# Stick-breaking weights turned in 32x32 blocks by VectorE and placed by ScalarE, in a two-layer streaming encoder

## The chip, the cores and the metric

The kernel runs on one NeuronCore of a Trainium2 chip. The metric is the device time of one execution, in microseconds (us); lower is better. In what follows PE is TensorE, DVE is VectorE, ACT is ScalarE, POOL is GpSimd and SP is SyncE.

## What is computed

Two layers over 512 tokens of width 2048, in float32. Layer A mixes a gated linear recurrence with an attention into 256 memory tokens; layer B mixes a stick-breaking attention of 12 heads (keys and values computed once, from the stream after layer A) with the same kind of memory attention. The change touches the stick-breaking attention alone:

```python
z = jnp.einsum('bhqd,bhkd->bhqk', q_blk, kh).astype(jnp.float32) * scale
log_beta = jax.nn.log_sigmoid(z)
log_keep = jnp.where(mask, jax.nn.log_sigmoid(-z), 0.0)
later = lax.cumsum(log_keep, axis=3, reverse=True) - log_keep
w = jnp.where(mask, jnp.exp(log_beta + later), 0.0)
return jnp.einsum('bhqk,bhkd->bhqd', w.astype(vh.dtype), vh)
```

The mask keeps keys that stand strictly before the query.

## The kernel before, in words

**Products.** A float32 product is made as three passes of PE (`three_passes`, L2126 to L2128) over operands that are each split in a high part (`..._hi`, written by ACT as a copy) and a low part (`..._lo`, the difference, written by DVE). Weights come from HBM in slabs of 512 rows by 512 columns, double-buffered: SP loads `w_raw`, ACT's `split` writes `w_hi` in two halves once the slab before the one that PE is in has been left (`slab_done`), DVE's `split` writes `w_lo`, and PE's `slab` waits for each piece (`lo_ready`) before its first of four token tiles. A slab on PE is four quarters (`t` 0 to 3) of 12 matmuls with 512 moving columns. Between quarters, `hooks` put other work on PE.

**The stick-breaking stage.** A loop of three turns (`Fori(0, NPAIR)`) runs eight slabs each, the gate columns and the next query columns of layer B's input projection, and beside them four heads: head `h` belongs to slabs (slots) `2h` and `2h+1`. For a head:

- `stick_scores` on PE writes the scores `z` of four query tiles to the PSUM tensor `aux`, tile `t` with its `128(t+1)` keys only. The first head's scores stand at quarter 1 of slot 0; those of the next heads stand straight behind the value products of the head ahead.
- ACT (L1222, L1223) writes `keep` and `beta`, the two sigmoids of `z`, for the four tiles.
- DVE (L1970 to L1977) masks the diagonal blocks, runs the reversed running product over `keep` and multiplies it into `beta`: these are the weights, with queries on partitions. `w_ready` counts the tiles.
- `stick_transposed` on PE (L2473) turns the ten 128x128 blocks of the weights that are not empty (four, three, two and one for the key blocks 0 to 3), into three banks of `aux`. It stands at quarter 1 (first head) or 0 (others) of the odd slot and raises `wt_done`.
- ACT (L1214) writes `wt_hi` from `aux` in pieces of 512, 512 and 256 columns, DVE (L1960) writes `wt_lo`.
- `stick_values` on PE (L2484), two quarters after the turn, waits for all of `wt_lo` and makes twelve products with the values, then the next head's scores follow.

**The order on ACT and DVE.** It is written out by hand and is the program's order; a wait holds all that stands behind it on its engine. In an even slot ACT first splits the next slab (waiting for PE's progress), then makes the head's eight sigmoids and issues the load of the next head's keys and values (`load_kv`); in slot 4 `gate_sigmoid` follows (L858, one instruction of 2048 columns). In an odd slot ACT makes `wt_hi`, then splits. DVE does the same in step: in an even slot `w_lo`, then the scan steps of the head; in an odd slot `wt_lo`, `w_lo`, then what the slot adds: in slots 3 and 7 the copies of the finished projection out of PSUM (`gate_out`, `branch_out`: L1514, L1510), in slot 5 the gate products, and in each odd slot the head's output after `o_done`.

**Sums of weights.** POOL, far from this stage's own data, makes sums of blocks of the output weights in HBM by accumulating DMAs (`move`, L621), counted in four semaphores `sums_made[n]`, one for each quarter `n` of this work; SP waits for them before it loads those sums.

## Time and profile before

| | |
|---|---|
| time, median of 3 runs | 1468.43 us (1468.14 to 1469.89) |
| span of the profiled execution | 1466.5 us |
| time of the profiled execution itself | not given apart from its span |
| PE busy | 1458.0 us, 99% of the span |
| DVE busy | 997.5 us, 68% |
| ACT busy | 716.3 us, 49% |
| the stick-breaking loop | three turns, one of them in the window of 1027 to 1134 us |
| PE, in the window of 1027 to 1134 us | 107.00 us busy of 107 |
| DVE, ACT in that window | 65.72 us, 38.42 us |

The span reaches from the first to the last instruction of the profiled execution; the runs' times hold also what lies around it, 1.9 us by the median. Busy time counts an engine as busy while any of its instructions is in flight. Matmuls overlap, so the duration of one is longer than the distance to the next; for PE the distance of the starts is what an instruction costs. In the chain of waits each piece of time belongs to what the end of the program waited for.

### The profile page before, as it was taken

What the parts mean: (1) busy time and instruction counts of PE and PEld (TensorE: products, weight loads), DVE (VectorE), ACT (ScalarE), POOL (GpSimd) and SP (SyncE); (2) the same over time, 40 slices, a digit from 0 to 9 for tenths busy, and PEclk for the clock granted to TensorE, in tenths of its full rate; (3) what the DMA queues carried; (4) which work ended last, traced back from release to release, by engine and by line L of the source; (5) the groups of instructions that cost most, each with busy time, mean ns of one, the idle gap of its engine ahead of it and who ended that gap; (6) DMA issues with size and microseconds to landing.
All of it is one profiled execution on the core that took longest, in us unless ns stands there. A gap on an engine that the chain in (4) does not pass through costs nothing.

```text
span 1466.5 us, 18207 instructions
## 1 busy us (share of the span) xinstructions
PE 1458.0 (99%) x6842; PEld 1221.7 (83%) x6842; DVE 997.5 (68%) x1317; ACT 716.3 (49%) x1066; POOL 122.8 (8%) x184
## 2 busy tenths in 40 slices
PE   9999999999999999999999999999999999999998
PEld 7888888888888888888888888888888888888886
DVE  6775568465576896856579676556566566578987
ACT  6764544444544645763325654433333433455465
POOL 0001111111110000000010001111111011000000
PEclk9999999999999999999999999999999999999999
DMA  9877788777886987477989876687888888858853
GB/s 344 290 287 225 159 215 228 174 235 158 212 251 165 323 323 260 155 262 282 358 326 372 291 224 219 244 218 196 230 241 244 202 239 208 226 188 329 315 200 144
DMA packets 154189, 357.97 MB, mean 244 GB/s; under 512 B 7824, under 2 KB 23440, under 8 KB 150032
## 3 DMA queue, kind: packets, MB, share of 16 engines
q1 hardware_dynamic: 103824, 205.98, 40.3%
q0 software_dynamic: 29376, 102.77, 28.3%
q10 hardware_dynamic: 20928, 48.41, 9.0%
q8 instruction: 38, 0.62, 0.2%
q14 instruction: 23, 0.19, 0.0%
HBM read 310.99 MB, written 113.25 MB: 289 GB/s over the span
## 4 chain that ended last, share of the span: by engine, by line
PE 99%; DMA 0%; SPq 0%; ACT 0%; issue 0%; DVE 0%; ACTq 0%
PE main L2128 25%; PE main L2127 25%; PE main L2126 25%; PE aux L2127 6%; PE aux L2126 6%; PE aux L2128 6%; PE aux L2484 2%; PE aux L2473 1%; DMA w_raw<-in_w_mem_kv 0%; PE aux L2270 0%; PE main L2178 0%; PE aux L2178 0%; PE main L2199 0%; PE main L2202 0%; PE main L2205 0%; PE aux L2220 0%
## 5 line engine op out<-in xcount | busy, mean ns | idle before, releaser
L2126 PE MATMUL main<-act_hi,w_hi 128*128 128x512 f32 x1216 | 475.3, 391 | 0.0
L2127 PE MATMUL main<-act_lo,w_hi 128*128 128x512 f32 x1216 | 473.6, 389 | 0.0
L2128 PE MATMUL main<-act_hi,w_lo 128*128 128x512 f32 x1216 | 473.6, 389 | 0.0
L2128 PEld LDWEIGHTS main<-act_hi,w_lo 128*128 128x128 f32 x1216 | 228.3, 188 | 47.4
L2127 PEld LDWEIGHTS main<-act_lo,w_hi 128*128 128x128 f32 x1216 | 228.4, 188 | 46.7
L2126 PEld LDWEIGHTS main<-act_hi,w_hi 128*128 128x128 f32 x1216 | 228.4, 188 | 46.4
L1334 DVE SCALAR_TENSOR_TENSOR w_lo<-w_raw,gains,w_hi 128x512 fp32r<-128x512 f32 x180 | 123.3, 746 | 120.5 <-ACT w_hi L704 120.5
L704 ACT ACTIVATE w_hi<-w_raw,gains 128x512 fp32r<-128x512 f32 x180 | 115.4, 712 | 140.6 <-PE main L2128 121.9
L1325 DVE TENSOR_TENSOR w_lo<-w_raw,w_hi 128x1024 fp32r<-128x1024 f32 x88 | 104.1, 1222 | 105.2 <-ACT w_hi L697 105.0
L697 ACT ACTIVATE w_hi<-w_raw 128x1024 fp32r<-128x1024 f32 x88 | 88.5, 1057 | 169.5 <-PE main L2128 132.7
L2126 PE MATMUL main<-w_hi,act_hi 128*128 128x512 f32 (+1 forms) x432 | 163.5, 378 | 0.0
L2127 PE MATMUL main<-w_lo,act_hi 128*128 128x512 f32 (+1 forms) x432 | 163.4, 378 | 0.0
L2128 PE MATMUL main<-w_hi,act_lo 128*128 128x512 f32 (+1 forms) x432 | 163.1, 377 | 0.0
L2126 PE MATMUL aux<-w_hi,act_hi 128*128 128x512 f32 (+1 forms) x348 | 129.4, 372 | 0.0
L2127 PE MATMUL aux<-w_lo,act_hi 128*128 128x512 f32 (+1 forms) x348 | 129.2, 371 | 0.0
L2128 PE MATMUL aux<-w_hi,act_lo 128*128 128x512 f32 (+1 forms) x348 | 128.9, 370 | 0.0
L2126 PEld LDWEIGHTS main<-w_hi,act_hi 128*128 128x128 f32 x432 | 81.3, 188 | 15.6
L2128 PEld LDWEIGHTS main<-w_hi,act_lo 128*128 128x128 f32 x432 | 81.2, 188 | 15.2
L2127 PEld LDWEIGHTS main<-w_lo,act_hi 128*128 128x128 f32 x432 | 81.3, 188 | 14.8
L755 ACT ACTIVATE w_hi<-work 128x1024 fp32r<-128x1024 f32 x56 | 56.3, 1053 | 64.2 <-issue 53.7
L755 ACT ACTIVATE w_hi<-w_raw 128x1024 fp32r<-128x1024 f32 x56 | 56.2, 1051 | 57.3 <-issue 57.3
L1372 DVE TENSOR_TENSOR w_lo<-w_raw,w_hi 128x1024 fp32r<-128x1024 f32 x56 | 66.2, 1220 | 25.7 <-ACT w_hi L755 25.6
(321 smaller groups left out, 1861.4 us busy)
## 6 DMA issues: line engine op xcount, KB each, us to landing
w_raw<-in_w_in_a SPq DMA_DIRECT2D x32, 1024.0 KB, 6.7
w_raw<-in_w_in_b SPq DMA_DIRECT2D x32, 1024.0 KB, 7.9
weight_sums<-in_w_out_a POOLq DMA_DIRECT2D x48, 512.0 KB, 7.0
weight_sums<-in_w_out_b POOLq DMA_DIRECT2D x48, 512.0 KB, 7.2
weight_sums<-weight_sums POOLq DMA_DIRECT2D x32, 512.0 KB, 6.4
w_raw<-weight_sums SPq DMA_DIRECT2D x16, 1024.0 KB, 6.6
work<-weight_sums SPq DMA_DIRECT2D x16, 1024.0 KB, 7.5
w_raw<-in_w_mem_kv SPq DMA_DIRECT2D x13, 1024.0 KB, 5.2
```

Of the source, the lines that this page charges most:

```text
L697: nc.scalar.activation(w_hi[:, j % 2, k:k + 2, :], raw[:, k:k + 2, :], ACT.Copy).then_inc(hi_ready, 2)
L704: nc.scalar.activation(w_hi[:, j % 2, k, :], raw[:, k, :], ACT.Copy, scale=s).then_inc(hi_ready, 1)
L755: nc.scalar.activation(w_hi[:, u % 2, k:k + 2, :], proj_raw[RAW[u]][:, k:k + 2, :], ACT.Copy).then_inc(hi_ready, 2)
L1325: V.tensor_tensor(w_lo[:, j % 2, k:k + 2, :], w_raw[:, j % 2, k:k + 2, :], w_hi[:, j % 2, k:k + 2, :].bitcast(F32), ALU.subtract).then_inc ...
L1334: V.scalar_tensor_tensor(lo, raw[:, k, :], gain[:, KS * j + k:KS * j + k + 1], hi, ALU.mult, ALU.subtract).then_inc(lo_ready, 1)
L1372: V.tensor_tensor(w_lo[:, u % 2, k:k + 2, :], proj_raw[RAW[u]][:, k:k + 2, :], w_hi[:, u % 2, k:k + 2, :].bitcast(F32), ALU.subtract).then ...
L2126: TE.matmul(o, a[0], b[0], start=first, stop=False)
L2127: TE.matmul(o, a[0], b[1], start=False, stop=False)
L2128: return TE.matmul(o, a[1], b[0], start=False, stop=final)
L2473: last = TE.transpose(o, beta[:, t, c:c + P], ident[:])
L2484: last = TE.matmul(aux[:, 0, P * k:T], v, w, start=(k, n) == order[0], stop=(k, n) == order[-1])
```

## The change

PE no longer turns the weights. For each head:

- DVE, straight behind the last scan step, issues four `transpose` instructions (one for each key block `k`, of 512, 384, 256 and 128 columns), each of which turns every 32x32 block of its input by itself and writes it to `turned`, 1280 columns in the place of `keep`.
- ACT waits for them (`wt_turned`) and then issues 16 copies, each of 32 partitions by 320 columns, which move group `r` of partitions and section `c` of columns of `turned` to partitions group `c` and section `r` of `placed`, 1280 columns in the place of `xr`.
- ACT's `wt_hi` and DVE's `wt_lo` read `placed` in place of the PSUM banks; `wt_hi` waits for all 16 copies (`wt_placed`).
- `stick_values` reads the same columns in another arrangement: its moving operand consists of runs of 32 columns with 320 columns from one run to the next (`turned_back`).
- For heads 1 to 3 of a turn the split of the next slab moves: on ACT from ahead of the sigmoids to between sigmoids and copies, on DVE from ahead of the scan steps to behind the four transposes. In slot 4 `gate_sigmoid` stands behind the copies.
- The four semaphores of POOL's sums become one, and POOL waits for all sums of quarter `n-1` before it starts those of quarter `n`.
- In slot 7 DVE has one more wait, on its own `wt_lo`.

The places of scores and values on PE stay as they were. The diff, cut to its core:

```diff
@@ -61,6 +61,7 @@
 WT_WIDTH = (512, 512, 256)
+TURN_AT = (0, 4, 7, 9)
 Z_ORDER = ((1, 3, 0), (0, 2, 384), (2, 2, 0), (3, 1, 0))
 F32 = mybir.dt.float32
@@ -208,6 +209,20 @@
         keep, beta = four(0), four(1)
         wt_hi = split_at("wt_hi", [P, 1280], 2)
         wt_lo = split_at("wt_lo", [P, 1280], 2, 1280)
+        turned = block(0)[:, 0:1280]
+        placed = work[:, 0:1280]
+
+        def turn_blocks(k):
+
+            at = XR + 2048 + 384 + 512 * k
+            src = work[:, at:at + 384 * (NT - k)].rearrange("p (t x) -> p t x", x=384)[:, :, 0:P]
+            dst = turned.rearrange("p (c n j) -> p n c j", c=4, j=32)[:, TURN_AT[k]:TURN_AT[k] + NT - k]
+            return dst, src.rearrange("p t (c i) -> p t c i", i=32)
+
+        def turned_back(w, k):
+
+            return w[:].rearrange("p (r n j) -> p n r j", r=4, j=32)[:, TURN_AT[k]:TURN_AT[k] + NT - k]
+
         ot = work[:, XR + 2048 * 2 + 2560:XR + 2048 * 2 + 3584].rearrange("p (b t) -> p b t", b=2)
         q_hi = split_at("q_hi", [P, 4, T], 6)
         q_lo = split_at("q_lo", [P, 4, T], 7)
@@ -548,7 +564,7 @@
...
-                sp.wait_ge(sums_made[2 * s], 16 * 32)
+                sp.wait_ge(sums_made, 16 * 32 * (2 * s + 1))
...
@@ -615,10 +631,10 @@
...
-            def move(n, dst, src, op):
+            def move(dst, src, op):
-                    pool.dma_start(dst[rows], src[rows], accum_op=op).then_inc(sums_made[n], 16)
+                    pool.dma_start(dst[rows], src[rows], accum_op=op).then_inc(sums_made, 16)
...
@@ -664,19 +680,21 @@
...
-                move(n, t1, b11, ALU.bypass)
-                move(n, t3, b12, ALU.bypass)
-                pool.wait_ge(sums_made[n], 16 * 8)
...
+                if n:
+                    pool.wait_ge(sums_made, 16 * 32 * n)
+                move(t1, b11, ALU.bypass)
+                move(t3, b12, ALU.bypass)
+                pool.wait_ge(sums_made, 16 * (32 * n + 8))
...
@@ -1209,11 +1227,13 @@
                         h, second = (4 * q + j) // 2, j % 2
                         n = 4 * i + h
                         if second:
-                            act.wait_ge(wt_done, n + 1)
+                            act.wait_ge(wt_placed, 16 * n + 16)
                             for b, w in enumerate(WT_WIDTH):
-                                nc.scalar.activation(wt_hi[:, 512 * b:512 * b + w], aux[:, 1 + b, 0:w], ACT.Copy
+                                part = slice(512 * b, 512 * b + w)
+                                nc.scalar.activation(wt_hi[:, part], placed[:, part], ACT.Copy
                                                      ).then_inc(wt_high, 1)
-                        split_next(G, j)
+                        if second or h == 0:
+                            split_next(G, j)
                         if not second:
                             for m, (t, bank, at) in enumerate(Z_ORDER):
                                 w = P * (t + 1)
@@ -1231,6 +1251,14 @@
                             else:
                                 load_kv((4 * i + 4) % NB, 0)
+                            if h:
+                                split_next(G, j)
+                            act.wait_ge(wt_turned, 4 * n + 4)
+                            for r in range(4):
+                                for c in range(4):
+                                    nc.scalar.activation(placed[32 * c:32 * c + 32, 320 * r:320 * r + 320],
+                                                         turned[32 * r:32 * r + 32, 320 * c:320 * c + 320], ACT.Copy
+                                                         ).then_inc(wt_placed, 1)
                         if 4 * q + j == 4:
                             gate_sigmoid(2 * i + (G_B + 1))
                         if 4 * q + j == 7:
@@ -1957,10 +1985,11 @@
                         if second:
                             for b, w in enumerate(WT_WIDTH):
                                 dve.wait_ge(wt_high, 3 * n + b + 1)
-                                V.tensor_tensor(wt_lo[:, 512 * b:512 * b + w], aux[:, 1 + b, 0:w],
-                                                wt_hi[:, 512 * b:512 * b + w].bitcast(F32), ALU.subtract
-                                                ).then_inc(wt_low, 1)
-                        split_next(G, j)
+                                part = slice(512 * b, 512 * b + w)
+                                V.tensor_tensor(wt_lo[:, part], placed[:, part],
+                                                wt_hi[:, part].bitcast(F32), ALU.subtract).then_inc(wt_low, 1)
+                        if second or h == 0:
+                            split_next(G, j)
                         if not second:
                             for m, (t, _, _) in enumerate(Z_ORDER):
                                 w = P * (t + 1)
@@ -1975,6 +2004,11 @@
                                                                   k[:, 1:w][:, ::-1], 1.0, ALU.mult, ALU.bypass))
                                 ch.wait(a3)
                                 V.tensor_tensor(b[:, 0:w - 1], b[:, 0:w - 1], k[:, 1:w], ALU.mult).then_inc(w_ready, 1)
+                            dve.wait_ge(w_ready, 4 * n + 4)
+                            for k in range(NT):
+                                V.transpose(*turn_blocks(k)).then_inc(wt_turned, 1)
+                            if h:
+                                split_next(G, j)
                         if slot == 3:
                             dve.wait_ge(y_stored, 16 * i + 64)
                             dve.wait_ge(v_stored[3], 64)
@@ -1985,6 +2019,7 @@
                             ch.link(V.tensor_tensor(block(4), block(4), block(5), ALU.mult))
                             V.tensor_tensor(gg[:, 0:2, :], gg[:, 0:2, :], ot[:, 0:2, :], ALU.mult)
                         if slot == 7:
+                            dve.wait_ge(wt_low, 12 * i + 12)
                             branch_out(G, 0)
                             branch_out(G, 1)
                         if second:
@@ -2463,24 +2498,13 @@
                     three_passes(aux[:, bank, at:at + w], (q_hi[:, h, P * t:P * t + P], q_lo[:, h, P * t:P * t + P]),
                                  (kv[:, h % 2, 0, 0:w], kv[:, h % 2, 1, 0:w])).then_inc(z_done, 1)
-            def stick_transposed(i, h):
-                pe.wait_ge(w_ready, 4 * (4 * i + h) + 4)
-                for k in range(NT):
-                    bank, at = ((1, 0), (2, 0), (3, 0), (2, 384))[k]
-                    for t in range(k, NT):
-                        o = aux[:, bank, at + P * (t - k):at + P * (t - k) + P]
-                        c = T - P * (t + 1) + P * k
-                        last = TE.transpose(o, beta[:, t, c:c + P], ident[:])
-                last.then_inc(wt_done, 1)
-
             def stick_values(i, h):
                 pe.wait_ge(wt_low, 3 * (4 * i + h) + 3)
                 order = [(0, 0), (0, 1), (0, 2), (3, 0), (1, 0), (3, 1), (1, 1), (3, 2), (1, 2), (2, 0), (2, 1), (2, 2)]
                 for k, n in order:
-                    at = (0, 512, 1024, 896)[k]
                     v = kv[:, h % 2, (2, 2, 3)[n], P * k:P * k + P]
-                    w = (wt_hi, wt_lo, wt_hi)[n][:, at:at + T - P * k]
+                    w = turned_back((wt_hi, wt_lo, wt_hi)[n], k)
                     last = TE.matmul(aux[:, 0, P * k:T], v, w, start=(k, n) == order[0], stop=(k, n) == order[-1])
                 last.then_inc(o_done, 1)
@@ -2498,8 +2522,7 @@
                             hooks = {1: lambda: stick_scores(i, 0)} if h == 0 else {}
                         else:
                             late = 1 if h == 0 else 0
-                            hooks = {late: lambda: stick_transposed(i, h),
-                                     late + 2: lambda: (stick_values(i, h), stick_scores(i, h + 1) if h < 3 else None)}
+                            hooks = {late + 2: lambda: (stick_values(i, h), stick_scores(i, h + 1) if h < 3 else None)}
                         slab(2 * i + (G_B + 1 + q), j, "T", hooks)
             mem_branch(1, G_B + 7)
```

How this moves instructions, at three places. First PE at quarter 1 of slot 1, before (L2467 is the wait for `w_ready`; `main` holds the slab's result):

```order
L2126 MATMUL main<-act_hi,w_hi 128x512
L2127 MATMUL main<-act_lo,w_hi 128x512
L2128 MATMUL main<-act_hi,w_lo 128x512
L2467 ISA
L2473 MATMUL aux<-ident,work 128x128 x10
L2126 MATMUL main<-act_hi,w_hi 128x512
L2127 MATMUL main<-act_lo,w_hi 128x512
L2128 MATMUL main<-act_hi,w_lo 128x512
```

The two rows in the middle go, at four places in the loop; nothing else on PE changes its place.

Second ACT between the sigmoids of head 2 (slot 4) and its `wt_hi` (slot 5), before:

```order
L1222 ACTIVATE work<-aux 128x512
L1223 ACTIVATE work<-aux 128x512
L1069 ISA
L1069 DMA kv<-kv_scratch 128x2048
L857 REGISTER_ALU
L858 ACTIVATE work<-work 128x2048
L1214 ACTIVATE wt_hi<-aux 128x512 x2
L1214 ACTIVATE wt_hi<-aux 128x256
```

and now:

```order
L1242 ACTIVATE work<-aux 128x512
L1243 ACTIVATE work<-aux 128x512
L1087 ISA
L1087 DMA kv<-kv_scratch 128x2048
L707 REGISTER_ALU
L712 ISA
L715 ACTIVATE w_hi<-w_raw 128x1024 x2
L1259 ACTIVATE work<-work 32x320 x16
L875 REGISTER_ALU
L876 ACTIVATE work<-work 128x2048
L1230 ISA
L1233 ACTIVATE wt_hi<-work 128x512 x2
```

The split of the slab (L715) came in from ahead of the sigmoids, the 16 copies (L1259) are new, and the gate's sigmoid (L876) and `wt_hi` stand behind them.

Third DVE at the end of slot 3 and the start of slot 4, before:

```order
L1514 TENSOR_TENSOR work<-main,rstd_bc 128x512
L1324 ISA
L1325 TENSOR_TENSOR w_lo<-w_raw,w_hi 128x1024
L1324 REGISTER_ALU
L1325 TENSOR_TENSOR w_lo<-w_raw,w_hi 128x1024
L1967 ISA
L1970 TENSOR_TENSOR work<-work,m_keep 128x128
```

and the end of the scan steps of that head now:

```order
L2006 TENSOR_TENSOR work<-work 128x511
L2009 STREAM_TRANSPOSE work<-work 128x4x4x32
L2009 STREAM_TRANSPOSE work<-work 128x3x4x32
L2009 STREAM_TRANSPOSE work<-work 128x2x4x32
L2009 STREAM_TRANSPOSE work<-work 128x4x32
L1352 ISA
L1353 TENSOR_TENSOR w_lo<-w_raw,w_hi 128x1024
```

The scan steps follow the gate product (L1514) at once, and `w_lo` of the slab (L1353) stands behind them and the four transposes.

## Rows read from the trace of the kernel before

**Rows 1.** The page: busy time by engine; granted TensorE clock; chain that ended last.

```profile
PE 1458.0 (99%) x6842; PEld 1221.7 (83%) x6842; DVE 997.5 (68%) x1317; ACT 716.3 (49%) x1066; POOL 122.8 (8%) x184
...
PEclk9999999999999999999999999999999999999999
...
PE 99%; DMA 0%; SPq 0%; ACT 0%; issue 0%; DVE 0%; ACTq 0%
```

**Rows 2.** Groups by line: count | busy us, mean ns | idle us before.

```profile
L2473 PE MATMUL aux<-ident,work 128*128 128x128 f32 x120 | 15.0, 272 | 0.0
```

**Rows 3.** Waits of 920 to 1260 us: total us, times, longest.

```profile
ACT wt_hi L1214 <- PE aux L2473: 83.2, 12, 7.9
```

**Rows 4.** Timeline of PE at the turn of head 0 (start, us long).

```profile
1049.69 0.39 PE L2128 MATMUL main<-act_hi,w_lo 128*128 128x512 f32 x1
1049.93 1.25 PE L2473 MATMUL aux<-ident,work 128*128 128x128 f32 x10
1050.94 0.48 PE L2126 MATMUL main<-act_hi,w_hi 128*128 128x512 f32 x1
1051.25 0.39 PE L2127 MATMUL main<-act_lo,w_hi 128*128 128x512 f32 x1
```

**Rows 5.** Timeline of PE: value products of the four heads begin; scores of head 2.

```profile
1056.49 0.39 PE L2484 MATMUL aux<-wt_hi,kv 128*128 128x512 f32 x1
...
1080.49 0.39 PE L2484 MATMUL aux<-wt_hi,kv 128*128 128x512 f32 x1
...
1082.38 0.28 PE L2126 MATMUL aux<-kv,q_hi 128*128 128x256 f32 x1
...
1107.21 0.39 PE L2484 MATMUL aux<-wt_hi,kv 128*128 128x512 f32 x1
...
1133.93 0.39 PE L2484 MATMUL aux<-wt_hi,kv 128*128 128x512 f32 x1
```

**Rows 6.** Timeline of DVE: steps of 255, 383, 511 columns, then wt_lo of head 0.

```profile
1042.39 0.42 DVE L1977 TENSOR_TENSOR work<-work 128x255 f32<-128x255 f32 x1
...
1045.18 0.56 DVE L1977 TENSOR_TENSOR work<-work 128x383 f32<-128x383 f32 x1
...
1047.31 0.69 DVE L1977 TENSOR_TENSOR work<-work 128x511 f32<-128x511 f32 x1
1051.85 1.62 DVE L1960 TENSOR_TENSOR wt_lo<-aux,wt_hi 128x512 fp32r<-128x512 f32 x3 [3.85 <-ACT wt_hi L1214]
```

**Rows 7.** Instructions of one line on ACT: duration ns min/median/max.

```profile
L796 ACT ACTIVATE act_hi<-f_raw x4: 402/402/417, 9.8 to 10.7; 128x256 fp32r<-128x256 f32 x4
```

**Rows 8.** Timeline of ACT: plain copies of 256 and of 512 columns, SBUF to SBUF.

```profile
9.80 1.34 ACT L796 ACTIVATE act_hi<-f_raw 128x256 fp32r<-128x256 f32 x4 [0.30 <-DMA f_raw<-in_mem_t]
...
1137.41 1.16 ACT L854 ACTIVATE q_hi<-work 128x512 fp32r<-128x512 f32 x2 [5.50 <-DVE work L1999]
1139.49 0.64 ACT L854 ACTIVATE q_hi<-work 128x512 fp32r<-128x512 f32 x1 [0.92 <-DVE work L1510]
```

**Rows 9.** Timeline of ACT: wt_hi of head 0, and the gate's sigmoid.

```profile
1051.22 1.36 ACT L1214 ACTIVATE wt_hi<-aux 128x512 fp32r<-128x512 f32 x3 [7.89 <-PE aux L2473]
...
1094.55 1.98 ACT L858 ACTIVATE work<-work 128x2048 f32<-128x2048 f32 x1
```

**Rows 10.** Timeline of DVE, head 2: gate product, w_lo, first and last scan step.

```profile
1089.96 0.69 DVE L1514 TENSOR_TENSOR work<-main,rstd_bc 128x512 f32<-128x512 f32 x1 [2.03 <-PE main L2128]
1091.27 2.37 DVE L1325 TENSOR_TENSOR w_lo<-w_raw,w_hi 128x1024 fp32r<-128x1024 f32 x2 [0.61 <-ACT w_hi L697]
1093.55 0.29 DVE L1970 TENSOR_TENSOR work<-work,m_keep 128x128 f32<-128x128 f32 x1
...
1099.59 0.69 DVE L1977 TENSOR_TENSOR work<-work 128x511 f32<-128x511 f32 x1
```

**Rows 11.** Timeline of POOL: the last sum issued for layer B.

```profile
1278.03 0.90 POOL L621 DMA_DIRECT2D weight_sums<-in_w_out_b  x1 [9.84 <-issue]
```

**Rows 12.** Timeline of SP: the first load behind its last wait for sums.

```profile
1360.15 6.24 SPq L533 DMA_DIRECT2D work<-weight_sums  x2
```

More of the change, by code:

```diff
@@ L397, in trunk @@
         w_ready = sem("w_ready")
-        wt_done = sem("wt_done")
+        wt_turned = sem("wt_turned")
+        wt_placed = sem("wt_placed")
         wt_high = sem("wt_high")
@@ L430, in trunk @@
         q22_loaded = [sem(f"q22_loaded{n}") for n in range(2)]
-        sums_made = [sem(f"sums_made{n}") for n in range(4)]
+        sums_made = sem("sums_made")
         sum_ready = sem("sum_ready")
@@ L562, in load_out @@
                     load_proj(s, u)
-                sp.wait_ge(sums_made[2 * s + 1], 16 * 32)
+                sp.wait_ge(sums_made, 16 * 32 * (2 * s + 2))
                 for u in range(14, N_PROJ):
@@ L666, in _ @@
                         store_value(m)
-                move(n, t1, b11, ALU.bypass)
-                move(n, t3, b12, ALU.bypass)
-                pool.wait_ge(sums_made[n], 16 * 8)
-                move(n, t1, b12, ALU.add)
-                move(n, t3, b22, ALU.add)
-                pool.wait_ge(sums_made[n], 16 * 16)
-                move(n, t2, t1, ALU.bypass)
-                pool.wait_ge(sums_made[n], 16 * 20)
-                move(n, t2, b22, ALU.add)
-                pool.wait_ge(sums_made[n], 16 * 24)
-                move(n, t4, t2, ALU.bypass)
-                pool.wait_ge(sums_made[n], 16 * 28)
-                move(n, t4, b21, ALU.add)
+                if n:
[3 more added lines that the diff above has]
+                pool.wait_ge(sums_made, 16 * (32 * n + 8))
+                move(t1, b12, ALU.add)
+                move(t3, b22, ALU.add)
+                pool.wait_ge(sums_made, 16 * (32 * n + 16))
+                move(t2, t1, ALU.bypass)
+                pool.wait_ge(sums_made, 16 * (32 * n + 20))
+                move(t2, b22, ALU.add)
+                pool.wait_ge(sums_made, 16 * (32 * n + 24))
+                move(t4, t2, ALU.bypass)
+                pool.wait_ge(sums_made, 16 * (32 * n + 28))
+                move(t4, b21, ALU.add)
         @blk.scalar
```

## The prediction

> **What bounds the kernel now.** I read the page first: PE is busy for 99% of the span, its granted clock is full in every slice, and the chain of waits that ends last is 99% PE [rows 1]. So there is one bound, the row of matmuls on PE. Time taken from PE comes off the end, and time in which PE stands still is added, since nothing behind it has slack of its own to give. DVE (68%) and ACT (49%) have room on the average, but an average tells nothing of one head: what counts is whether the chain through them ends before PE asks for its result. So I read the groups by line for what PE gives up, the waits for what happens around the turn of the weights, and then the timelines of PE, DVE and ACT through one turn of the loop (the second; the others repeat it).
>
> The waits show 83.2 us of ACT idling for PE's transposes, 12 times, up to 7.9 us [rows 3]. That is the slack of the old arrangement: the weights of a head were ready early, and ACT waited until PE came to its hook. The new chain has to fit in there.
>
> **What the change removes.** 120 transposes, ten for each of 12 heads [rows 2]. The mean of 272 ns is latency, not cost; the starts tell the cost [rows 4]. A 512-column product starts at 1049.69 and the turn 0.24 later; the turn lasts 1.01 until the next product starts, and that one holds up its successor by 0.31 instead of 0.24. So a turn costs PE 1.08 us, and 12 of them **13.0 us**. This part is sure, if PE does not wait.
>
> **What it adds, instruction by instruction.**
> - Four block transposes on DVE, of 512, 384, 256 and 128 columns. No row shows one. The nearest are DVE's own one-pass steps in SBUF: 0.69 us for 511 columns, 0.56 for 383, 0.42 for 255 [rows 6], 0.29 for 128 [rows 10]. I take these in full, 1.96 us for each head. The lower bound lets neighbours overlap, as the three `wt_lo` do (0.69 + 0.69 + 0.42 would be 1.80, they take 1.62 [rows 6]), 1.69; the upper bound is a second pass over float32, 3.9.
> - 16 copies on ACT of 32 partitions by 320 columns. By the nearest rows partitions cost nothing and columns do. A 256-column copy lasts 0.40 [rows 7], four take 1.34, so one starts 0.31 behind the other; with 512 columns one lasts 0.64 and two take 1.16, so 0.52 apart [rows 8]. A quarter of the way between: 0.36 apart, 0.46 for the last, 15 x 0.36 + 0.46 = **5.9 us** for each head. Upper bound: no overlap, 16 x 0.46 = 7.3. Lower bound: the slope alone, 0.21 us for 256 columns or 0.26 for 320, is 4.4.
> - `wt_hi` to the end of `wt_lo`: 1051.22 to 1053.47, 2.25 us [rows 6, 9]. Reading SBUF instead of PSUM changes it by under 0.1.
> - Handovers: `wt_lo` starts 0.63 after `wt_hi` [rows 6, 9], hardly more than a piece of 512 columns lasts; I put 0.04 for each, an estimate, 0.12 for three.
>
> All pieces of this chain are in series: DVE, ACT, ACT, DVE, then PE's wait for `wt_lo`. What hides it is the work of PE between a head's scores and its values. I now walk through one turn of the loop, in the times of before; PE comes to each value product 1.08 earlier.
>
> *Head 0* has the shortest cover (six quarters of a slab). Scan steps end at 1047.31 + 0.69 = 1048.00 [rows 6]. Then 1.96 + 5.90 + 2.25 + 0.12 = 10.23: ready at 1058.23. PE asks at 1056.49 - 1.08 = 1055.41 [rows 5]. **PE waits 2.8 us.**
>
> *Head 1*: scores from 1058.38; with about 1 us to the first sigmoids and the 6.73 us of scan steps that head 2 shows (1093.55 to 1100.28 [rows 10]) ready at 1076.4; PE asks at 1080.49 - 1.08 = 1079.4 [rows 5]. 3 us spare, no wait.
>
> *Head 2*: its scores come at 1082.38 [rows 5], but DVE is held by the last gate product of slot 3, which waits for the slab's end: 1089.96 + 0.69 = 1090.65. Before, `w_lo` came next and the scan steps began at 1093.55 [rows 10]; now they begin at 1090.65, a gain of 2.9. 6.73 + 1.96 + 5.90 gives 1105.24. Then ACT has the gate's sigmoid in front of `wt_hi`, 1.98 [rows 9], which used to lie in idle time. With 2.25 + 0.12: 1109.59. PE asks at 1107.21 - 1.08 = 1106.13 [rows 5]. **PE waits 3.5 us.** The moved split is the other edge here: `w_lo` for slab 5 stands behind the transposes, so its first half (2.37/2) ends at 1090.65 + 6.73 + 1.96 + 1.19 = 1100.5. PE enters that slab two quarters before it asks for the values; a quarter is 2.73 (1082.38 to 1107.21, less a turn, 1.08, and the scores, taken as long as the value products, 1.9; that by eight), so at 1100.7. It just fits; anything that DVE's transposes take beyond their price is a wait there.
>
> *Head 3*: same distance on PE (1107.21 to 1133.93 [rows 5]), no gate sigmoid, and PE itself is 3.5 later: about 3 us spare.
>
> What else moves: the earlier issue of the keys' load only helps. POOL's new waits cost a landing each; its last sum for layer B is issued at 1278.03 [rows 11] and the first load behind SP's wait at 1360.15 [rows 12], so 80 us cover it. The new wait in slot 7 is on work that DVE itself finished. All three are costed at nothing.
>
> **Sum:** 3 x (2.8 + 3.5) = 18.9 added, 13.0 removed: **+5.9 us**. Against the span of 1466.5 this is 1472.4; the median of the runs is 1.9 above the span, and 1468.4 + 5.9 = **1474.3 us**.
>
> **A rule weighed against the rows.** ACT's copies change the first partition of their input every fourth time and that of their output each time; no row of this trace starts anywhere but at partition 0, so the overlap that I took is not shown for them. The Trainium skill (VectorE: DVE Perf Modes, section on two Vector instructions with no wait between them) says that a Vector instruction whose operands start in another group of 32 partitions than those ahead begins only when all earlier ones have finished. It says this of Vector and not of Scalar; if it held there too, the sum would be that of the first rival, and by the rule's silence it is the one above.
>
> **Rivals.**
> 1. *The copies do not overlap.* Each starts when the one ahead has ended: 7.3 in place of 5.9 us, 1.43 more in both tight heads, 8.6 in all, and still inside the 3 us of the other two. +14.5, 1482.9. For it: nothing else separates the pieces, and the unoverlapped duration is only 0.1 above the distance that I took. Against it: each overlapped pair in the rows. Chance 0.27.
> 2. *DVE's transposes take two passes.* 1.96 more on the same two heads (in head 2 as a wait for slab 5 first): 11.8, so +17.7, 1486.1. Chance 0.10.
> 3. *The chain fits: faster.* If a copy costs by its slope alone, since a quarter of the partitions is written, the 16 take 4.4. Break-even of the whole change is when the two waits of a turn sum to 13.0/3 = 4.3 instead of 6.3, that is 1.0 less in each chain; with 1.5 less the sum is 18.9 - 9.0 - 13.0 = -3.1, 1465.3. Against it: the fixed part is in each row of ACT. Chance 0.05.
> 4. *Waits shrink to a tie.* Chain shorter by 0.5 to 1.4 (some overlap of transposes, copies nearer to 0.31 apart): within 0.2%. Chance 0.13, with the low end of my own case.
> 5. *The clock falls behind the waits.* Before, PE never stands still in this stage and the granted clock is full [rows 1]. If each of six waits were followed by a quarter of a slab at the lower level, 2.7 us more each: +22, 1490. The Trainium skill (TensorE: Matmul & The Clock Gate, Part 1) has the clock drop after PE has been idle, which speaks against a change that trades PE work for PE waits; no row here shows it. Chance 0.06.
> 6. *The strided moving operand runs at half rate.* A head's value products last 1.89 (1080.49 to 1082.38 [rows 5]); 12 x 1.89 = 22.7, so +28.6, 1497. Chance 0.05.
>
> That the transposes stay on PE can be excluded from the instruction order. My own case keeps 0.34.
>
> **How the numbers follow.** Faster by over 0.2% (2.9 us, about what a measurement of this kernel can tell from no change) is rival 3: 0.05. Within it is rival 4: 0.13. The rest is slower: 0.82. The likeliest time is my own case, 1474.3; its own range, with transposes from 1.69 to 2.5 and the copies' bounds not touched, is 1472 to 1478. The range of 8 in 10 takes in rival 1 with half of rival 2 on top and half of rival 4: 1469 to 1489. It leaves out rivals 3, 5 and 6 and the rest of 4, about 0.2.
>
> **What would show it.** Right: no PE rows of L2473's kind; PE idle in front of the value products of heads 0 and 2 of each turn, about 2.8 and 3.5 us, put down to `wt_lo`; none in front of heads 1 and 3; 16 copies over 5.9 us; four transposes over about 2 us; slab 5 entered without a wait. Copies 0.46 apart mean rival 1. Wrong: PE busy throughout with a span below 1464; waits at heads 1 or 3; a granted clock below full; value products further apart than 0.24 us for 512 columns.

## The result, and the profile after

| | before | after |
|---|---|---|
| median | 1468.53 us (4 runs, beside those of after) | 1495.74 us (4 runs, 1495.26 to 1496.74) |
| span of the profiled execution | 1466.5 us | 1493.4 us |
| mean granted TensorE clock | 0.999 | 0.990 |

The ratio is 1.0184, 95% interval 1.017 to 1.0199: **27.2 us slower** by the medians, 26.9 by the spans. The sign was forecast; the size was not, and the time lies 6.7 us above the range. The page of after, its lines on busy time, the chain that ended last and the costliest new group:

```profile
PE 1456.4 (98%) x6722; PEld 1218.1 (82%) x6722; DVE 1016.5 (68%) x1365; ACT 809.7 (54%) x1258; POOL 122.8 (8%) x184
...
PE 89%; ACT 4%; DVE 3%; issue 2%; DMA 0%; SPq 0%; DVEq 0%; ACTq 0%
...
L1259 ACT ACTIVATE work<-work 32x320 f32<-32x320 f32 x192 | 90.0, 469 | 57.5 <-DVE work L2009 53.1
```

Against [rows 1], the 120 transposes are gone from PE's count, yet its busy time fell by 1.6 us only: something else on PE became longer. The chain, 99% PE before, now runs through ACT and DVE for 7% of the span.

The waits between 920 and 1280 us, in which all twelve heads lie (waiting instruction <- released by: us in total, times, longest):

```profile
DVE wt_lo L1989 <- ACT wt_hi L1233: 88.3, 12, 8.6
ACT work L1259 <- DVE work L2009: 53.1, 12, 7.0
PEld aux L2508 <- DVE wt_lo L1989: 30.5, 6, 5.3
...
PE aux L2508 <- DVE wt_lo L1989: 28.0, 6, 4.9
```

ACT's wait for PE [rows 3] has gone. In its place PE waits for `wt_lo`, six times for nearly 5 us. Which six, the timelines tell. ACT and DVE at head 0 and head 2 of the second turn (start, us long, how many, idle before), ACT first:

```profile
1058.18 7.86 ACT L1259 ACTIVATE work<-work 32x320 f32<-32x320 f32 x16 [6.44 <-DVE work L2009]
1066.07 1.46 ACT L1233 ACTIVATE wt_hi<-work 128x512 fp32r<-128x512 f32 x3
...
1112.12 7.87 ACT L1259 ACTIVATE work<-work 32x320 f32<-32x320 f32 x16 [6.95 <-DVE work L2009]
1120.02 1.91 ACT L876 ACTIVATE work<-work 128x2048 f32<-128x2048 f32 x1
1121.83 1.44 ACT L1233 ACTIVATE wt_hi<-work 128x512 fp32r<-128x512 f32 x3
```

```profile
1056.45 1.69 DVE L2009 STREAM_TRANSPOSE work<-work 128x512 f32<-128x512 f32 x4
1066.73 1.63 DVE L1989 TENSOR_TENSOR wt_lo<-work,wt_hi 128x512 fp32r<-128x512 f32 x3 [8.58 <-ACT wt_hi L1233]
```

From the first transpose to the end of `wt_lo` head 0 takes 1068.36 - 1056.45 = 11.9 us, 7.9 of them the 16 copies. And PE, which wanted the result at 1063.79:

```profile
1063.56 0.39 PE L2163 MATMUL main<-act_hi,w_lo 128*128 128x512 f32 x1
1068.41 0.80 PE L2508 MATMUL aux<-wt_hi,kv 128*128 128x512 f32 x1 [4.47 <-DVE wt_lo L1989]
1069.01 0.63 PE L2508 MATMUL aux<-wt_lo,kv 128*128 128x512 f32 x1
...
1071.89 0.42 PE L2508 MATMUL aux<-wt_hi,kv 128*128 128x256 f32 x1
1072.10 0.42 PE L2161 MATMUL aux<-kv,q_hi 128*128 128x256 f32 x1
```

PE stands still for 4.6 us, and then its value products take 1072.10 - 1068.41 = 3.69 us instead of 1.89 [rows 5]. The table of windows (stretch and its length; busy time and count of PE, PEld, DVE, ACT, POOL; granted clock; DMA share; GB/s) shows why:

```profile
1064.00:1066.00 2.00, 0.00 (x0) 0.00 (x0) 0.00 (x0) 1.91 (x5) 0.00 (x0) 1.00 0.81 111
1066.00:1068.00 2.00, 0.00 (x0) 0.00 (x0) 1.27 (x3) 1.97 (x5) 0.00 (x0) 0.57 0.71 127
1068.00:1070.00 2.00, 1.58 (x5) 1.30 (x5) 1.79 (x4) 1.42 (x2) 0.89 (x1) 0.50 0.00 0
1070.00:1072.00 2.00, 2.00 (x10) 2.00 (x9) 0.93 (x1) 0.00 (x0) 0.00 (x0) 0.50 0.82 54
1072.00:1074.00 2.00, 2.00 (x12) 1.97 (x12) 1.02 (x3) 0.68 (x3) 0.00 (x0) 0.72 1.03 173
1074.00:1076.00 2.00, 2.00 (x10) 1.64 (x9) 1.93 (x7) 2.00 (x6) 0.00 (x0) 1.00 1.01 327
```

The granted clock falls to 0.50 of full speed, that is from 2.4 to 1.2 GHz, in the stretch in which PE is idle, stays there through the value products, and comes back while the scores run.

Read off the starts of PE's rows, for each head of the three turns (the wait, then the time of the value products, then of the next head's scores; "none" is within 0.01):

| | wait | values | scores behind them |
|---|---|---|---|
| before, all heads | none | 1.89 to 1.90 | 1.91 to 1.92 |
| after, head 0 | 4.63, 4.62, 4.64 | 3.16, 3.69, 3.69 | 2.34, 2.38, 2.39 |
| after, head 1 | none | 1.91 | 1.91 |
| after, head 2 | 5.00, 5.01, 5.01 | 3.57, 3.58, 3.56 | 1.92 |
| after, head 3 | none | 1.92 | other work |

The waits sum to 28.9 us, what the products take over their old times to 11.3, and 13.0 were saved: 28.9 + 11.3 - 13.0 = **+27.2**. The spans differ by 26.9 and the medians by 27.2, so nothing else of more than 0.3 us is needed to explain the difference. In what follows the same sum ("waits + slow products - 13.0") is held against each kernel's span less 1466.5.

### The profile page after: what moved, and what is told of

Its sections match the earlier page's. It is cut to its first block, busy times and chain, and to the rows that moved or that the text cites. A ratio compares the mean times of both kernels' runs of the same rounds, so it can differ in the third digit from the quotient of the medians.

```text
span 1493.4 us, 18210 instructions
## 1 busy us (share of the span) xinstructions
PE 1456.4 (98%) x6722; PEld 1218.1 (82%) x6722; DVE 1016.5 (68%) x1365; ACT 809.7 (54%) x1258; POOL 122.8 (8%) x184
## 4 chain that ended last, share of the span: by engine, by line
PE 89%; ACT 4%; DVE 3%; issue 2%; DMA 0%; SPq 0%; DVEq 0%; ACTq 0%
PE main L2162 22%; PE main L2161 22%; PE main L2163 22%; PE aux L2161 6%; PE aux L2162 6%; PE aux L2163 6%; ACT work L1259 3%; PE aux L2508 2%; DVE work L2003 1%; DMA w_raw<-in_w_mem_kv 0%; PE aux L2305 0%; DVE work L2009 0%; DVE work L1999 0%; DVE work L2006 0%; DVE wt_lo L1989 0%
## 5 line engine op out<-in xcount | busy, mean ns | idle before, releaser
L1353 DVE TENSOR_TENSOR w_lo<-w_raw,w_hi 128x1024 fp32r<-128x1024 f32 x88 | 103.7, 1217 | 67.4 <-ACT w_hi L715 67.3
L715 ACT ACTIVATE w_hi<-w_raw 128x1024 fp32r<-128x1024 f32 x88 | 88.1, 1049 | 103.6 <-PE main L2163 65.0
L1259 ACT ACTIVATE work<-work 32x320 f32<-32x320 f32 x192 | 90.0, 469 | 57.5 <-DVE work L2009 53.1
L2161 PEld LDWEIGHTS main<-w_hi,act_hi 128*128 128x128 f32 x432 | 81.3, 188 | 15.4
```

The lines of the kernel that those rows point to most:

```text
L715: nc.scalar.activation(w_hi[:, j % 2, k:k + 2, :], raw[:, k:k + 2, :], ACT.Copy).then_inc(hi_ready, 2)
L1259: nc.scalar.activation(placed[32 * c:32 * c + 32, 320 * r:320 * r + 320], turned[32 * r:32 * r + 32, 320 * c:320 * c + 320], ACT.Copy).the ...
L1353: V.tensor_tensor(w_lo[:, j % 2, k:k + 2, :], w_raw[:, j % 2, k:k + 2, :], w_hi[:, j % 2, k:k + 2, :].bitcast(F32), ALU.subtract).then_inc ...
L2161: TE.matmul(o, a[0], b[0], start=first, stop=False)
```

## The experiments

Two things stood open: why a copy costs 0.49 instead of 0.36 us, and whether the lower clock is the cause of the slow products or goes with something else. Each experiment is an edit of the changed kernel, except for the sixth. Their runs of the kernel before had medians of 1468.34 to 1468.77 us.

**1. Copies that stay in their group of partitions.** (`placed` then doesn't hold the turned weights: the placement is left out.)

```diff
-for r in range(4):
-    for c in range(4):
+for c in range(4):
+    for r in range(4):
         nc.scalar.activation(placed[32 * c:32 * c + 32, 320 * r:320 * r + 320],
-                             turned[32 * r:32 * r + 32, 320 * c:320 * c + 320], ACT.Copy
+                             turned[32 * c:32 * c + 32, 320 * r:320 * r + 320], ACT.Copy
```

> Each of the 16 copies stays in its own group of 32 partitions (group c to group c), with c in the outer loop, so input and output change their group only at every fourth copy; size, number and semaphores are those of the change. This kernel leaves out the move across partition groups. Theory (a copy whose start partition differs from that of the copy ahead begins only when that one has ended): 12 of 16 copies start about 0.36 us behind the one ahead and 4 about 0.49, the 16 take 6.2 to 6.5 us instead of 7.87, PE's waits at heads 0 and 2 of a turn shrink from 4.63 and 5.0 to about 3.1 and 3.5 us; with the slow value products left as they are (11.3 us) the time is 1486, without them 1475. Rival (copies of 32 partitions are 0.49 us apart whatever their groups): all as in the change, 1495.7.

1484.16 us (1481.81 to 1486.32), ratio 1.0105 [1.0088, 1.0121]. The same number of copies of the same size, on the timeline of ACT, and their durations (min/median/max ns):

```profile
1053.33 6.27 ACT L1259 ACTIVATE work<-work 32x320 f32<-32x320 f32 x16 [6.44 <-DVE work L2009]
```

```profile
L1259 ACT ACTIVATE work<-work x192: 447/453/472, 942.6 to 1251.0; 32x320 f32<-32x320 f32 x192
```

6.27 us instead of 7.87. The starts of the single copies in this trace tell more than the sum: the three steps of the 15 that still change group are 0.48 apart, the first step behind a change 0.38 and all others 0.36, the very distance that the prediction took. No copy of this kernel carries data from one group to another, so what makes a step long is that its groups are not those of the copy ahead, and not that data crosses from group to group. So the 0.13 us by which each copy was priced too low come from the change of partition group. The waits are 3.04 and 3.41 us, and after these the clock does not always fall: it fell behind each of the three waits of head 0 (3.04 to 3.05 us), with products of 3.01 to 3.68 us, and behind only one of the three longer ones of head 2 (3.41 us; 3.68 us there, 2.02 and 2.04 in the other turns). 19.3 + 9.4 - 13.0 = 15.7, the span shows 15.4.

**2. The loops exchanged, work unchanged.** Now the output stays in its group for four copies and the input changes each time.

```diff
-for r in range(4):
-    for c in range(4):
+for c in range(4):
+    for r in range(4):
```

> The same 16 copies as the change, with the loops exchanged: the output group changes at every fourth copy, the input group at each. Theory in its full form (a change of either start partition holds the copy): all 0.49 us apart as in the change, span 1493.4. If only the output's group counts: 12 of 16 are 0.36 apart, 16 take about 6.3 us, span 1473 to 1484. Rival (32 partitions alone make it slow): no difference from the change.

A single run: 1497.76 us, span 1495.6. The order of the loops is that of experiment 1, so the order is not what helped there. The copies take 7.86 us as in the change, the waits sum to 28.94. So it doesn't help to keep one side still: a change on the input side holds the copy as much as one on the output side. Its slow products cost 13.4 instead of 11.3, which is the whole difference of span (29.3 worked out, 29.1 shown); the clock's return isn't the same from kernel to kernel.

**3. The gate's sigmoid ahead of the copies.** In head 2 ACT had it between the copies and `wt_hi`.

```diff
+if h == 2:
+    gate_sigmoid(2 * i + (G_B + 1))
 act.wait_ge(wt_turned, 4 * n + 4)
 ...
-if 4 * q + j == 4:
-    gate_sigmoid(2 * i + (G_B + 1))
```

> In slot 4 the gate's sigmoid (1.9 us) stands in front of ACT's wait for the transposes, where ACT idles 6.95 us in the change, instead of behind the copies. PE's wait at head 2 falls from 5.0 to 3.1 us, three times: 5.7 us. Theory that the slow products behind a wait come from the clock that PE's idling lowers: with 3.1 us of wait the clock falls later or not at all, and up to 1.69 more each time come back, so 1485 to 1490. Rival (the products are slow because their moving operand is strided): they stay 3.57 us long and the time is 1490.0; but heads 1 and 3, with the same operand and no wait, took 1.91.

1486.75 us (1485.98 to 1487.93), ratio 1.0123 [1.0106, 1.014]. Head 2 waits 3.21 to 3.23 us instead of 5.0, and its products take 2.02 to 2.04: behind these waits the clock stayed up, three times of three. PE and the windows at head 2 of the second turn (the clock is the third figure from the end):

```profile
1120.05 0.50 PE L2508 MATMUL aux<-wt_hi,kv 128*128 128x512 f32 x1 [3.07 <-DVE wt_lo L1989]
```

```profile
1118.00:1120.00 2.00, 0.00 (x0) 0.00 (x0) 1.63 (x3) 2.00 (x4) 0.43 (x1) 1.00 0.15 61
1120.00:1122.00 2.00, 1.95 (x12) 1.82 (x13) 1.80 (x2) 1.05 (x2) 0.71 (x2) 1.00 0.46 74
```

24.0 + 7.3 - 13.0 = 18.3; the spans show 18.2. The order of one instruction of 1.9 us is worth 9 us.

**4. Four copies instead of sixteen.** Three quarters of the placement are left out.

```diff
-for r in range(4):
+for r in range(1):
     for c in range(4):
         ...
-                ).then_inc(wt_placed, 1)
+                ).then_inc(wt_placed, 4)
```

> Only the 4 copies of the first input group are issued, each counted fourfold; the other 12 are left out, so this kernel leaves out three quarters of the placement and its weights are not all there. The chain is 5.9 us shorter, more than either wait. Theory (PE's waits and the clock behind them are all that the change adds, PE's transposes all that it takes away): no wait on PE in this stage, granted clock full, value products 1.9 us long, 1468.5 - 13.0 = 1455.5. A rival cost elsewhere (the single semaphore of POOL's sums, the strided operand, the moved split) would leave it above that by its size.

1455.48 us (1455.09 to 1455.91), ratio 0.991 [0.9893, 0.9926], clock 0.999. 1468.5 - 13.0 = 1455.5: with no wait left the whole saving of the transposes is in the time, and transposes on DVE, the moved splits, POOL's and SP's new waits and the strided operand together cost nothing that can be measured. PE at the border of slab and head 0:

```profile
1050.17 0.39 PE L2163 MATMUL main<-act_hi,w_lo 128*128 128x512 f32 x1
1050.40 0.40 PE L2508 MATMUL aux<-wt_hi,kv 128*128 128x512 f32 x1
1050.63 0.40 PE L2508 MATMUL aux<-wt_lo,kv 128*128 128x512 f32 x1
```

**5. The copies shared between ACT and DVE, gate's sigmoid first.** Nothing is left out: DVE makes eight of the sixteen, behind its split in heads 1 to 3 (below, first ACT's lines, then DVE's; the gate's sigmoid moves as in experiment 3).

```diff
+PIECES = [(r, c) for r in range(4) for c in range(4)]
-for r in range(4):
-    for c in range(4):
+for r, c in PIECES[:8]:
 ...
+dve.wait_ge(wt_turned, 4 * n + 4)
+for r, c in PIECES[8:]:
+    V.tensor_copy(placed[32 * c:32 * c + 32, 320 * r:320 * r + 320],
+                  turned[32 * r:32 * r + 32, 320 * c:320 * c + 320]
+                  ).then_inc(wt_placed, 1)
```

> Gate's sigmoid first, as in the run before with that name, and the 16 copies shared: the first 8 on ACT, the last 8 on DVE, there behind the transposes (heads 1 to 3: behind the slab's split). Theory: at head 0 the placement takes 8 x 0.49 = 3.9 us instead of 7.9, the wait of 4.7 falls to about 0.7; at head 2 it ends with DVE, 2.3 (split) + 8 x 0.4 = 5.5 us behind the transposes, and the wait of 3.2 falls to about 0.8. Six waits of under 1 us are 4.5 in all, too short for the clock to fall: 1468.6 - 13.0 + 4.5 = 1460, faster than both kernels. Rival (DVE pays more for a change of partition group than ACT, 0.6 us or more for a copy): waits of 1.5 to 3 us, 1465 to 1475.

1460.32 us (1459.14 to 1460.9), ratio 0.9935 [0.9919, 0.9952]: faster than both. The groups by line, and then the timelines of DVE and of ACT at head 1 (the distances are the same in every head):

```profile
L1261 ACT ACTIVATE work<-work 32x320 f32<-32x320 f32 x96 | 45.1, 470 | 54.8 <-DVE work L2009 52.7
L2014 DVE COPY work<-work 32x320 f32<-32x320 f32 x96 | 30.8, 320 | 3.0
```

```profile
1067.37 2.78 DVE L2014 COPY work<-work 32x320 f32<-32x320 f32 x8
```

```profile
1065.13 3.94 ACT L1261 ACTIVATE work<-work 32x320 f32<-32x320 f32 x8 [2.75 <-DVE work L2009]
```

ACT's copies are 0.49 apart and 0.47 long; DVE's are 0.35 apart and 0.32 long. DVE starts 2.2 us later, since its split stands in front. On neither engine does the next one start before the one ahead has ended. Waits of 0.70 in head 0 and 0.4 in head 2, no fall of the clock: 3.2 + 0.8 - 13.0 = -9.0; the span shows -8.2.

**6. The sums' single semaphore alone,** put into the kernel before.

```diff
-sums_made = [sem(f"sums_made{n}") for n in range(4)]
+sums_made = sem("sums_made")
 ...
+if n:
+    pool.wait_ge(sums_made, 16 * 32 * n)
-pool.wait_ge(sums_made[n], 16 * 8)
+pool.wait_ge(sums_made, 16 * (32 * n + 8))
 ...
```

> The kernel before with one part of the change alone: POOL's sums counted in one semaphore, with its new waits. Both theories expect no difference: 1468.5 within 0.2%. If it is slower, the placement's part of the loss is smaller by that.

1468.45 us (1467.91 to 1469.04), ratio 0.9993 [0.9984, 1.0003]: nothing, as the prediction had it.

**7. PE kept busy in its waits.** 18 products ahead of the values of heads 0 and 2, into a bank whose scores have been read, so that nobody reads their result. The chain on ACT and DVE is untouched.

```diff
+def fill_wait(i, h, count):
+    pe.wait_ge(z_read, 4 * (4 * i + h) + 4)
+    for _ in range(count):
+        TE.matmul(aux[:, 1, :], kv[:, h % 2, 0, 0:P], kv[:, h % 2, 0, :], start=True, stop=True)
 ...
+if h % 2 == 0:
+    fill_wait(i, h, 18)
```

> The change, with 18 products of 512 columns (about 4.1 us) put on PE in front of the value products of heads 0 and 2, into a PSUM bank whose contents nobody needs any more; they fill most of the waits of 4.63 and 5.0 us and leave the chain as it is. Clock theory: the granted clock stays full, value products last 1.9 us at all heads, the 11.3 us of slow products go and the waits stay, 1484.4 us, although PE has more to do. Rival (the products behind a wait are slow for their operand or because they have just been released): 1495.7 or more.

1485.64 us (1485.41 to 1486.21), ratio 1.0111 [1.0094, 1.0128], clock 0.999. PE at head 0:

```profile
1060.47 4.24 PE L2505 MATMUL aux<-kv 128*128 128x512 f32 x18
1065.30 0.50 PE L2516 MATMUL aux<-wt_hi,kv 128*128 128x512 f32 x1 [0.59 <-DVE wt_lo L1989]
1065.64 0.40 PE L2516 MATMUL aux<-wt_lo,kv 128*128 128x512 f32 x1
```

and the windows of that stretch, columns as above:

```profile
1062.00:1064.00 2.00, 2.00 (x10) 1.65 (x10) 0.38 (x1) 1.94 (x4) 0.00 (x0) 1.00 0.85 150
1064.00:1066.00 2.00, 1.41 (x7) 0.85 (x6) 1.78 (x4) 2.00 (x4) 0.22 (x1) 1.00 0.03 6
```

The value products still begin 4.83 us (5.02 in head 2) behind the slab, hardly later than in after; but they take 2.04 instead of 3.69 us, and the time falls by 10.1 against after. So the slow products come from the clock, and the clock from PE's idleness; data that arrives late, or the strided operand, has no part in it beyond the 0.13 us by which 2.04 exceeds 1.91. That remainder and the slightly longer waits are why the time is 1.2 us above the 1484.4 expected.

**8. Shares set by head.** The shared version, with 7 copies on ACT and 9 on DVE in head 0, and 9 and 7 in the others.

```diff
-for r, c in PIECES[:8]:
+for r, c in PIECES[:9 if h else 7]:
 ...
-for r, c in PIECES[8:]:
+for r, c in PIECES[9 if h else 7:]:
```

> The shared version (gate sigmoid first, 8 copies on each engine) with the shares set by head: 7 copies on ACT and 9 on DVE in head 0, 9 and 7 in the others. In the shared version ACT's 8 copies take 3.93 us (0.49 apart) and DVE's 8 take 2.78 (0.35 apart). Head 0: both start together and ACT ends last, so one copy less on ACT ends the chain 0.49 earlier: PE's wait falls from 0.70 to about 0.2. Head 2: DVE starts 2.3 later, behind its split, and ends last, so one less there ends it 0.35 earlier: the wait falls from 0.40 to about 0.05. Sum 3 x 0.85 = 2.5 us less than the shared version: 1457.8, ratio about 0.9925. Theory (the copies' distances on each engine set the chain, PE's waits set the time): 1457 to 1458.5. Rival (the shorter waits and the slower products of 0.12 us behind them are a fixed cost of any handover, not of the chain's length): no change, 1460.

1457.13 us (1456.3 to 1457.54), ratio 0.9923 [0.991, 0.9937], the best of all and within 1.7 us of the limit that experiment 4 sets. Waits of 0.22 to 0.23 in head 0 and 0.03 to 0.15 in head 2, together 0.97. That is 2.2 us less than with equal shares; the medians differ by 3.2. The two profiled spans, 1458.3 and 1454.2, tell where the rest lies: from the slab's end at the first head to the value products of the last head the trace is 2.3 us shorter, as the waits say; the other 1.8 us lie ahead of that stretch (1.1) and behind it (0.7), where the two kernels are the same. So they are not the copies' doing; what made them is open. What remains behind even the shortest wait is 0.11 to 0.13 us in the value products: in experiment 7 the second starts 0.34 behind the first, in experiment 4 0.23.

**9. The split back ahead of sigmoids and scans.** The other half of the diff: in before the next slab's split stood first in each slot, and the change moved it behind the transposes for h > 0.

```diff
-if second or h == 0:
-    split_next(G, j)
+split_next(G, j)
 ...
-if h:
-    split_next(G, j)
```

(on ACT and on DVE)

> The change without its moved split: ACT and DVE split the next slab ahead of sigmoids and scan steps for all heads, as before. Theory (the chain of a head is what PE waits for): at heads 1 and 3 the scan steps begin about 7 us later, when the slab's split is done, which takes their spare time of 1 to 2 us and makes PE wait about 6 us; at head 2 they begin 2.9 us later and the wait grows from 5.0 to about 8. Some 15 us for each of three turns, with slow products behind six more waits: 1540 to 1560. Rival (the split's place matters little, since ACT and DVE have room on the average): within 5 us of 1495.7.

A single run: 1560.24 us, span 1558.1, clock 0.971, at the top of what was expected. The waits from 920 to 1330 us:

```profile
PEld aux L2502 <- DVE wt_lo L1986: 78.6, 12, 8.2
PE aux L2502 <- DVE wt_lo L1986: 73.5, 12, 7.8
```

Now all twelve heads wait: head 0 as in after 4.6, head 1 6.3 to 6.5, head 2 8.0, head 3 6.2, with the clock down behind each. 75.4 + 26.5 - 13.0 = 88.9; the spans differ by 91.6. The rest lies behind head 3, where no scores follow: there the next five products of the slab also run at the lower clock, 0.43 instead of 0.23 us apart, 3.0 us in the three turns, which the sum leaves out. The reordering that came with the change is what keeps heads 1 and 3 free.

## Why the prediction was wrong in size

**Right, with its measure.** *PE's saving of 13.0 us*: experiment 4 shows 13.2 by its medians. *Which heads wait*: 0 and 2 of each turn, never 1 and 3. *The transposes*: four in 1.69 us, the lower bound, not the 1.96 taken; rival 2 (two passes) is out. *Slab 5*: entered without a wait. *`wt_hi` to the end of `wt_lo`*: 1066.07 to 1068.36, 2.29 against 2.25. *The gate's sigmoid*: in front of `wt_hi`, worth 1.8 us of wait in experiment 3. *The strided operand*: 1.91 to 1.92 instead of 1.89, so rival 6 is out. *POOL and SP*: nothing in experiment 6, and in after the load behind SP's wait starts at

```profile
1387.07 6.24 SPq L549 DMA_DIRECT2D work<-weight_sums  x2
```

which is 26.9 us later than in [rows 12], just what the span has grown by.

**The first term that failed: "16 copies, 0.36 apart, 5.9 us".** Measured: 0.493 apart, 7.87 us, 2.0 more. Less what the transposes took less (0.27) that makes the waits 4.5 and 5.2 instead of 2.8 and 3.5, close to the 4.6 and 5.0 of the table; and 28.9 instead of 18.9 us in all, **10.0 of the 21.3 us that were missing**. The working of the size was good: where the partition group stays the same, the copies are 0.36 apart (experiment 1), although the rows that it came from all have 128 partitions and the copies have 32. What failed was to carry an overlap seen only between operands at partition 0 over to operands that change their partitions. The prediction had seen this, as its rival 1, and gave it 0.27. What it did not see is that even "no overlap" was short: it took the duration of an overlapped copy, 0.46, as the distance, where each copy now lasts 0.469 and the next starts 0.02 later, so its upper bound of 7.3 us (16 x 0.46 is nearer 7.4) was none. The Trainium skill (VectorE: DVE Perf Modes, section on two Vector instructions with no wait between them) states the hold for Vector alone; experiments 1 and 2 show the same on Scalar, for inputs and for outputs, each by itself. To read a rule's silence on the other engine as its absence was the weak point.

**The second: the clock at nothing.** Rival 5, with a chance of 0.06 and a price of 16 us over its own case, was right in kind: each of six waits is followed by a lower clock. Its price was too high, since the low clock lasts over the value products and part of the scores, not for a quarter of a slab: 1.9 us for each wait on the average instead of 2.7, 11.3 us in all, **the other half of the miss**. The Trainium skill (TensorE: Matmul & The Clock Gate, Part 1) has the clock drop after idleness, and here the trace agrees: granted 0.50 behind 4.6 us, and experiment 7 takes it away by work that does nothing. The prediction weighed it by the lack of a row; but in this stage before has no wait of PE, so its rows there could not have shown it either way.

**The two are not independent,** and that was the error in the range. The prediction priced its rivals one at a time. A longer chain makes longer waits, and behind waits as long as these the clock fell each time: from 4.6 us upwards always (after, experiments 2, 3 and 9). Below that the length alone doesn't tell: 3.2 us without a fall, three of three (experiment 3), 3.0 with one, three of three, and 3.4 with one in one of three (experiment 1); what decides there is open. Rival 1 alone would have ended at 1482.9; with the 11.3 us of the clock behind it the sum is 1494.2, 1.5 from what was measured. A range that took rival 1 in had to take in what its waits set off.

**Its break-even was right.** It put the change at zero where the two waits of a turn sum to 4.3 us. With 1.1 (experiment 5) the kernel is 8 us faster; with 9.85 and no fall of the clock (experiment 7) it is 17 us slower, where 3 x 9.85 - 13.0 gives 16.6. It holds only while the clock stays up: in experiment 1 the two waits sum to 6.45, which by this rule is 6.3 us slower, and the span is 15.4 longer.

## What to carry to other kernels

Before work is moved off a bounding engine, lay the new chain against the time at which that engine asks for its result, head by head; 13 us saved were lost three times over in six waits, while the same copies, shared between two helpers and with the gate's sigmoid out of the chain, left the kernel 11 us faster than before. Price small copies whose partition group changes from one to the next by their full duration and 0.02 to 0.03 us more on ACT as on DVE (0.49 for 0.47, 0.35 for 0.32 here), not by the distance of neighbours that stay at partition 0. Count a wait of several microseconds on TensorE as the wait plus the slower products behind it, and price rivals that cause one another together.

## What the runs showed of the hardware that was not expected

- ACT's copies of 32 partitions by 320 columns are 0.49 us apart (0.47 long) when the group of 32 partitions of input or output is another than in the copy ahead, and 0.36 apart (0.45 long) when both stay. DVE's are 0.35 apart (0.32 long) with a change; without one no run shows them.
- The granted clock can fall to half during a wait of PE (0.57 between 1066 and 1068 us, with PE idle from 1063.8), or only as the wait ends: at head 2, idle from 1119.2 to 1124.16, the windows show

```profile
1122.00:1124.00 2.00, 0.00 (x0) 0.00 (x0) 1.52 (x3) 2.00 (x4) 0.00 (x0) 1.00 0.91 227
1124.00:1126.00 2.00, 1.84 (x5) 1.56 (x6) 1.79 (x3) 1.17 (x2) 0.68 (x2) 0.58 0.11 43
```

- Waits of 3.0 us were followed by the lower clock in all three turns of experiment 1, waits of 3.4 in one of three there, and waits of 3.2 in none of experiment 3, so at these lengths the price can't be told from the length.
- Every wait whose clock stayed full, even one of 0.03 us, was followed by value products of 2.02 to 2.04 instead of 1.91 us.
- Block transposes of float32 on DVE cost no more than other steps of their size: four of 512, 384, 256 and 128 columns take 1.69 us.
